# Moving the modulation jobs of the shared gated layers from the down products to the gate/up steps

## The reference

```python
def swiglu(x, w13, w2):
    a, b = jnp.split(x @ w13, 2, axis=-1)
    return (jax.nn.silu(a) * b) @ w2

def ffn_half_step(h, g, shift, scale, gate, w13, w2):
    return h + 0.5 * gate * swiglu(modulate(rms_norm(h, g), shift, scale), w13, w2)
...
        m = jnp.split((silu_c @ w_ada[i] + b_ada[i])[:, None, :], N_MOD, axis=-1)
        mc = jnp.split((silu_cc @ w_ada[i] + b_ada[i])[:, None, :], N_MOD, axis=-1)
        h = ffn_half_step(h, g_ffn1[i], m[0], m[1], m[2], w13_ffn1[i], w2_ffn1[i])
        hc = ffn_half_step(hc, g_ffn1[i], mc[0], mc[1], mc[2], w13_ffn1[i], w2_ffn1[i])
```

## Time and profile before

| | us |
|---|---|
| median of 3 runs | 3689.54 (3684.26 to 3697.37) |
| span of the profiled execution | 3679.9 |
| time of the profiled execution outside the span | not in the profile; median less span is 9.6 |
| PE busy in the span | 3511.9 (95%) |
| DVE busy | 2154.9 (59%) |
| ACT busy | 1032.2 (28%) |
| POOL busy | 133.0 (4%) |
| sums of the modulation jobs on DVE, L2605 and L2602 | 622.8 and 98.4 |

### The profile page before, as it was taken

How to read it: one execution, slowest core, us unless ns; L and a number is a source line. 1 busy time by engine, 2 the same in 40 slices (tenths; PEclk the granted TensorE clock), 3 DMA queues, 4 the chain that set the end, 5 groups by cost and what they waited for, 6 DMA issues and landing times. The chain is left out here.

```text
span 3679.9 us, 49835 instructions
## 1 busy us (share of the span) xinstructions
PE 3511.9 (95%) x20487; PEld 2893.2 (79%) x20487; DVE 2154.9 (59%) x5075; ACT 1032.2 (28%) x1604; POOL 133.0 (4%) x116
## 2 busy tenths in 40 slices
PE   7998989999999999899999999989999999999998
PEld 5755868887888888774688888878888887578887
DVE  7555566557666565854455657575656636543334
ACT  3454023223321212333432121222121124432222
POOL 0012010000000000100000000010000010000000
PEclk9998889999999999998999999999999999999999
DMA  6532034443324342420123434333333323023331
GB/s 181 148 87 61 3 98 118 123 119 111 89 84 115 93 120 82 118 68 12 32 67 91 117 91 115 93 97 86 104 102 97 107 56 101 20 69 98 92 102 64
DMA packets 637196, 333.92 MB, mean 91 GB/s; under 512 B 21891, under 2 KB 633191, under 8 KB 636712
## 3 DMA queue, kind: packets, MB, share of 16 engines
q1 hardware_dynamic: 636612, 330.60, 31.9%
q10 hardware_dynamic: 356, 0.14, 0.0%
HBM read 328.57 MB, written 2.77 MB: 90 GB/s over the span
## 5 line engine op out<-in xcount | busy, mean ns | idle before, releaser
L2078 PE MATMUL psum<-hn_high,high 128*128 128x512 f32 (+1 forms) x3136 | 1128.3, 360 | 8.4 <-DVE low L2522 8.4
L2080 PE MATMUL psum<-hn_high,low 128*128 128x512 f32 (+1 forms) x3136 | 1111.9, 355 | 0.0
L2079 PE MATMUL psum<-hn_low,high 128*128 128x512 f32 (+1 forms) x3136 | 1108.5, 353 | 0.0
L2078 PEld LDWEIGHTS psum<-hn_high,high 128*128 128x128 f32 x3136 | 593.4, 189 | 110.6 <-issue 16.7
L2080 PEld LDWEIGHTS psum<-hn_high,low 128*128 128x128 f32 x3136 | 591.5, 189 | 87.5
L2079 PEld LDWEIGHTS psum<-hn_low,high 128*128 128x128 f32 x3136 | 592.6, 189 | 84.7 <-issue 0.5
L2605 DVE SCALAR_TENSOR_TENSOR partial<-stage,cond,partial 128x128 f32<-128x128 f32 x2304 | 622.8, 345 | 0.0
L2522 DVE TENSOR_TENSOR low<-stage,high 128x1024 fp32r<-128x1024 f32 (+2 forms) x415 | 493.4, 1209 | 179.4 <-ACT high L1759 178.9
L1759 ACT ACTIVATE high<-stage 128x1024 fp32r<-128x1024 f32 (+2 forms) x415 | 415.3, 1025 | 516.2 <-DMA stage<-in_w_ffn 373.3
L2078 PE MATMUL psum<-hidden_high,high 128*128 128x512 f32 (+1 forms) x1408 | 500.7, 356 | 1.6 <-DVE hidden_low L2527 1.5
L2080 PE MATMUL psum<-hidden_high,low 128*128 128x512 f32 (+1 forms) x1408 | 494.5, 351 | 0.0
(11 more groups left out here) (314 smaller groups left out, 3167.5 us busy)
## 6 DMA issues: line engine op xcount, KB each, us to landing
stage<-in_w_ffn SPq DMA_DIRECT2D x240, 512.0 KB, 4.3
stage<-in_w_ada SPq DMA_DIRECT2D x192, 512.0 KB, 4.0
stage<-in_w_in SPq DMA_DIRECT2D x48, 512.0 KB, 5.3
stage<-in_w_out SPq DMA_DIRECT2D x24, 512.0 KB, 4.2
stage<-in_w_ffn SPq DMA_DIRECT2D x32, 384.0 KB, 4.2
stage<-in_w_gate SPq DMA_DIRECT2D x22, 512.0 KB, 3.9
stage<-in_w_up SPq DMA_DIRECT2D x22, 512.0 KB, 5.1
stage<-in_w_down SPq DMA_DIRECT2D x16, 512.0 KB, 4.1
```

The costliest lines, as they stand in the source:

```text
L2078: self.e.matmul(out, high[:, i], xh, start=first and n == 0, stop=False)
L2079: self.e.matmul(out, high[:, i], xl, start=False, stop=False)
L2080: done = self.e.matmul(out, low[:, i], xh, start=False, stop=last and n == nk - 1)
```

## The change

In a layer with two parts, the down steps no longer take a modulation job. Each gate/up step but the first takes a second one, in the turn of the last part: in PE's queue behind the context's products, in DVE's behind the gating of the sequence and ahead of the gating of the context. In layers with one part nothing changes. All the diff:

```diff
@@ -1191,6 +1191,8 @@
                         self.products(("up_sum", key), bank_b.ap[:, 0:T], n_b, wb, part.hn, 0, [])
                     if n == len(parts) - 1:
                         self.pump()
+                        if n and at:
+                            self.pump_background()
                     t = self.temps.next()
                     high, low = hidden[n]
                     self.gated_tile(key, bank_a.ap[:, 0:T], bank_b.ap[:, 0:T], t, t.ap[:, 0:T], high[:, f, :], low[:, f, :],
@@ -1200,8 +1202,6 @@
                 slot_a.free = slot_b.free = [last]
             for f in range(KT):
                 n_d, slot, view = self.weights(w_down, first * P, tiles, f * P)
-                if len(parts) > 1:
-                    self.pump_background()
                 for n, part in enumerate(parts):
                     bank = self.banks.next()
                     key = name, first, f, n
```

## The result

The changed kernel takes 3757.76 us (median of 3 runs, 3757.49 to 3766.46), the kernel before 3686.90 (4 runs): ratio 1.020, 95% interval 1.0184 to 1.0216. The change costs 2.0%; 3752 was forecast, within 3712 to 3785. The span of the profiled execution grew from 3679.9 to 3755.5 us, by 75.6.

A forecast was written before the change was run, and what follows sets the result against it. TensorE (PE), busy 95% of the span, bounds the kernel; in two-job steps the load loop decides. 94−51−7+15+12 = +63 on 3679.9 gives 3743, plus 9.6 outside the span 3752 us, 1.7% slower; range 3712 to 3785, chance 0.70.

The forecast's parts named there:

- gate/up steps of the shared layers, clock included: Steps with two jobs: +94 us for 9 at 18.03, 43 at 19.0 and scalings; +12 us for clock falls.
- down products: Down products of the shared layers without jobs: −16, −10 and −25 us by group, together −51 us.
- tails: What follows the last down product: −3.7 us in the first shared layer, −3.3 in the second, together −7 us.
- three forced jobs, with the clock: Before the second shared layer three missing jobs run in a row with PE idle: +15 us, bounds 0 and 20.
- the loop of the loads: Second sums, next loads on SP, split, first sums, gating, second sums: 19.0 us a step, longer than PE's 18.03.
- first pair of a group: First two-job step of a gate/up group: 18.03 us, its gate block loaded early; 0.66 more behind a scaling.
- rival (a): Loads are not in the gate/up loop: 18.03 us for all steps, +9 us, 3699 us; chance 0.12.
- (c): Second sums end before PE reaches the next step: each of 61 steps pays 0.42 us, 3672 us; chance 0.05.
- (d): The change does less than it says: three forced jobs, 61 instead of 64 pairs, already in the sum; no chance given.
- every second one: Clock falls counted in every second of the 43 middle gate/up steps: 43×0.28 = +12 us, bounds 0 and +65.
- rival (b): Clock falls in every step or longer, or second loads take 6.7 us: +25 to +60, about 3790; chance 0.13.
- 9.6 us added for the time outside the span: Added to the predicted span of 3743 us, from the runs' median of 3689.54, to give 3752 us.

The follow-up runs named there:

- e2: Changed kernel, but the second job of a shared gate/up step reads the resident identity tile and takes no load or stage: 3702.95 us, ratio 1.0040.
- e6: Changed kernel, but both jobs' sums stand at the step's head and PE takes both up behind the context's products: 3665.72 us, ratio 0.9941.
- e7: e6 plus three jobs kept in down steps of the first shared layer's second group, so none is forced: 3653.67 us, ratio 0.9908.
- e3: Changed kernel with nine 128x256 products, results unused, on PE between the take-ups of the two jobs' sums: 3751.90 us, ratio 1.0173.

## Why the prediction was right

Point by point, in spans of the profiled executions, with sums over the three shared layers. Gate/up steps are taken from the first product of 128x512 of a layer, or the first of a group, to the first down product:

| term | forecast | measured |
|---|---|---|
| gate/up steps of the shared layers, clock included | +94 and +12 | +119.7 (1108.9 to 1228.7) |
| down products | −51 | −51.7 (603.1 to 551.4) |
| tails | −7 | −7.3 |
| three forced jobs, with the clock | +15 | +12.9 in their stretch |
| elsewhere | none | +2.0 |
| all | +63 | +75.6 |

**The place and order of the work** decided, as said, and the loop of the loads was the longer of the two. The first pair of a group came out at 17.92 to 18.28 us (forecast 18.03; 18.66 where a scaling stands ahead of it, forecast 18.69), the middle ones at a median of 19.00 where the clock stayed up (forecast 19.0), and rival (a), in which the loads are not in the loop, did not hold for the changed kernel. Rivals (c) and (d) didn't hold either.

**The mis-sized term** is the one of the gate/up steps with the clock, +106 forecast and +119.7 measured. Over 17.10 us a step, the 9 first steps of groups cost 9.0 us (forecast 9.0), the 43 middle ones 102.2 (forecast 97.0, clock and scalings included) and the 9 last ones 8.4 (forecast nothing).

Most of the miss is in those last steps. The prediction had them at 17.10 us, since the down products don't wait for the last sums, and that is right: four of them measure 17.10. But it counted the clock for the middle steps alone. PE waits at the head of a last step like at any other, and the clock fell behind 5 of these 9 waits; in such a step PE has nothing more to wait for, so no loop hides the loss and it shows in full, 1.4 to 2.4 us. One of them, in which PE is busy all through:

```profile
1490.11:1508.59 18.48, 18.48 (x102) 16.03 (x102) 12.63 (x38) 3.83 (x6) 0.00 (x0) 0.91 0.34 93
```

In the middle steps the clock was sized about rightly: 15 spells at 0.74 us each make 11, for 12. Nor was the "every second one" a bad guess: outside the first group of the first shared layer 11 of the 12 middle steps with a spell were followed by a short stretch without large products (1.40 to 1.62 us) and no spell, as the prediction argued. The rest of the 102.2 us is mostly late loads: in the five longest middle steps without a spell, 19.92 to 21.01 us, the gate block took 6.12 to 6.61 us to land. Of 51 blocks of layer weights that were issued right behind a block of `w_ada`, 9 took over 6 us to land (the changed kernel, to the end of the shared layers); before the change it was 5 of 54, so it isn't shown that the change made such loads more frequent. A load that lands late cost nothing while it was hidden; inside the loop it shows in full. One such step of the changed kernel, 20.10 us with the clock at 1.00, and its load:

```profile
1251.64:1271.74 20.10, 17.70 (x106) 15.63 (x106) 13.99 (x43) 3.82 (x6) 0.00 (x0) 1.00 0.38 106
...
stage<-in_w_ffn SPq DMA_DIRECT2D x1, 512.0 KB, 6.3
```

So a small part of rival (b), which gave 25 to 60 us more, was at work beside the forecast. The Trainium skill (TensorE: Matmul & The Clock Gate, "HAM oscillation — how this bites in real kernels") describes a loop with a wait for a load in every tile, in which every tile starts at the low clock. The trace of the changed kernel doesn't agree as a whole: 15 of 43 middle steps had a spell. In the first group of e2 it does: all six steps with a wait at their head had one.

**The forced jobs** cost 12.9 us in their stretch (7.09 to 19.96) and 12 us between e6 and e7, for +15; the bounds of 0 and 20 held.

**Luck.** The forecast of 3752 us is nearer to the measured 3757.8 than its terms are: they come to +63, where the spans differ by 75.6 and the medians by 70.9. The 9.6 us added for the time outside the span are not that time. In every run on record the time exceeds the span by about 2 us (3757.49 for 3755.5 here, 3681.84 for 3679.9 in the profiled execution of the kernel before); the other 7.7 us are there because the profiled execution of the kernel before was one of its shorter runs. With 2 us the same terms give 3745, still inside the range.

The down products gained what removing the waits and 0.42 us a job gives, and e6 and e7 keep that gain, with the tails: e6 has 1137.4 us of these gate/up steps, +28.5 on the kernel before, for 61 more jobs in them.

## What to carry to other kernels

Side work that is moved must be followed on every in-order queue it stands in: here the number of jobs in a step was harmless, the place of one of them put its result in front of the next step on TensorE and its load in front of the weights on SP. Ask of each load what the one ahead of it in the queue waits for. Here four stages for four blocks a step tied the next load of a second job to the end of the second sums, and the weights behind it with it; that is read from the order of issue (another number of stages was not tried), and e6 shows that the same ring does no harm when the last consumer is done early. A loss that a longer loop hides in the middle of a group shows in full in its last step. And count the jobs against the next hard deadline: three too few cost 12 us.

## What the runs showed of the hardware

A load of 512 KB that is issued 0.42 us behind another takes about 5.2 us to land (median of the 51 pairs above in the changed kernel), and 9 of these 51 took over 6 us. Why those take longer was not tried.

In e3, PE's wait filled with products took 16 of 20 spells of the low clock away. What PE did before the clock fell can be read for every step of the changed kernel with a job at its head and two in the step before: from the start of the last large product to the start of the next, the 20 spells had stretches of 2.06 to 4.61 us in front of them. No spell followed the 19 shorter stretches, 1.40 to 1.75 us. But 13 more stretches were of 2.17 us or longer and had none, while in e2 six on end of 2.06 to 2.27 us each had one. What tells those apart stays open.
